# Delta-rule work ahead of the RWKV outputs, and the delta matrix in a weight slab

## What is computed

```python
cols = split_columns(rms_norm_2(x, norm_g[layer]) @ w_in[layer])
y_gdn = gdn_branch(...)     # 6 heads, both directions, chunks: (I + A) U = rhs, then outputs
y_mla = mla_branch(...)     # 6 heads of softmax attention with rotary parts
y_rwkv = rwkv7_branch(...)  # 4 heads, both directions, a linear recurrence
mix = concatenate([y_gdn, y_mla, y_rwkv]) * silu(cols['gate'])
x = x + mix @ w_out[layer]
```

```python
a_mat = beta[..., :, None] * einsum('nhcid,nhcjd->nhcij', k, k) * d_strict
sol = triangular_solve(a_mat, rhs, left_side=True, lower=True, unit_diagonal=True)
p_intra = einsum('nhcid,nhcjd->nhcij', q, k) * d_incl
```

## Time and profile before

| | |
|---|---|
| median of 3 timed runs | 1298.87 us (1296.49 to 1302.06) |
| span of the profiled execution | 1293.0 us; its time with what lies around the span was not recorded |
| TensorE matmul | 1229.4 us busy, 95% |
| VectorE | 755.1 us, 58% |
| ScalarE | 345.7 us, 27% |
| GpSimd | 51.8 us, 4% |
| mean granted TensorE clock | 0.992 of full |

### The profile page before, as it was taken

The page is one execution under the profiler, slowest core; times in us unless marked ns, Lnnn a source line. Parts: engine busy times, 40 slices in busy tenths (PEclk is TensorE's granted clock), DMA queues, the critical chain, the costliest instruction groups (busy, mean ns, idle before and its releaser), DMA issues. The chain is left out here.

```text
span 1293.0 us, 18502 instructions
## 1 busy us (share of the span) xinstructions
PE 1229.4 (95%) x7285; PEld 878.9 (68%) x7285; DVE 755.1 (58%) x1471; ACT 345.7 (27%) x748; POOL 51.8 (4%) x92
## 2 busy tenths in 40 slices
PE   6999899999999999999999999989899999998997
PEld 5877549995447674699844478658566686575683
DVE  3244456775352145676743549884884378858872
ACT  2253312120012144121100222334441231334422
POOL 1100000000000000000000000200300000203000
PEclk9999999999999999999999999999999999999999
DMA  9731105454553431353544433310010632300000
GB/s 296 256 120 66 65 18 207 167 183 146 192 188 126 143 130 66 131 194 136 193 177 151 176 116 130 130 67 2 1 51 1 205 138 81 131 2 1 2 2 33
DMA packets 65853, 149.25 MB, mean 115 GB/s; under 512 B 2097, under 2 KB 8135, under 8 KB 65767
## 3 DMA queue, kind: packets, MB, share of 16 engines
q1 hardware_dynamic: 62432, 141.63, 30.9%
q0 software_dynamic: 1216, 3.52, 1.0%
q10 hardware_dynamic: 2119, 2.91, 0.9%
HBM read 146.95 MB, written 1.07 MB: 114 GB/s over the span
## 5 line engine op out<-in xcount | busy, mean ns | idle before, releaser
L1366 ACT ACTIVATE region<-banks 128x384 f32<-128x384 f32 (+8 forms) x159 | 77.0, 484 | 306.9 <-PE banks L442 105.0
L442 PE MATMUL banks<-hnT,weight_slabs 128*128 128x256 f32 x576 | 126.6, 380 | 3.4 <-DVE hnT L1842 3.4
L442 PEld LDWEIGHTS banks<-hnT,weight_slabs 128*128 128x128 f32 x576 | 108.8, 190 | 20.1 <-DVE hnT L1842 4.1
L494 PE MATMUL banks<-weight_slabs,region 128*128 128x512 f32 x256 | 115.1, 592 | 0.0
L494 PEld LDWEIGHTS banks<-weight_slabs,region 128*128 128x128 f32 x256 | 48.5, 190 | 60.3 <-issue 60.3
L494 PE MATMUL banks<-region 128*128 128x512 f32 x192 | 87.6, 592 | 0.0
L1825 DVE TENSOR_TENSOR region<-weight_slabs 128x1024 f32<-128x1024 f32 x32 | 39.2, 1225 | 80.3 <-PE banks L494 76.4
L1825 DVE TENSOR_TENSOR region<-region 128x256 f32<-128x256 f32 (+23 forms) x160 | 75.8, 474 | 16.9 <-ACT region L1712 11.8
L1983 DVE TENSOR_TENSOR region<-banks,region 128x128 f32<-128x128 f32 x40 | 11.7, 292 | 117.8 <-PE banks L609 91.2
L1825 DVE TENSOR_TENSOR region<-weight_slabs,region 128x1024 f32<-128x1024 f32 x64 | 78.2, 1222 | 1.1
L1322 POOL TENSOR_TENSOR region<-region,consts 128x240 f32<-128x240 f32 (+24 forms) x60 | 34.4, 598 | 955.3 <-DVEq L1834 934.2
(11 more groups left out here) (365 smaller groups left out, 2056.5 us busy)
## 6 DMA issues: line engine op xcount, KB each, us to landing
weight_slabs<-in_mlp_w SPq DMA_DIRECT2D x32, 2048.0 KB, 8.9
weight_slabs<-in_w_in SPq DMA_DIRECT2D x10, 2048.0 KB, 7.7
weight_slabs<-in_od_w_in SPq DMA_DIRECT2D x6, 2048.0 KB, 7.9
weight_slabs<-in_ev_w_in SPq DMA_DIRECT2D x4, 2048.0 KB, 10.9
weight_slabs<-in_w_out SPq DMA_DIRECT2D x4, 2048.0 KB, 8.1
weight_slabs<-in_ev_w_out SPq DMA_DIRECT2D x2, 2048.0 KB, 8.3
weight_slabs<-in_od_w_out SPq DMA_DIRECT2D x2, 2048.0 KB, 7.8
weight_slabs<-in_w_in SPq DMA_DIRECT2D x2, 2016.0 KB, 7.6
```

What stands on the lines that cost most here:

```text
L442: ins = mm(view(ps, b + i * S, (1, S)), view(slabs, o + k * width + c0, (1, P)), view(hnT, k * S, (1, S)), start=k == 0, stop=k == KC - 1)
L494: ins = mm(view(ps, b, (1, 512)), view(R, act + k * st, (1, P)), view(w, wt + k * step_, (1, 512)), start=n == 0 and k == 0, stop=n == 7 a ...
L1366: say(A(dst, view(ps, b, *(dims or ((1, n),)), np_=np_), ACT.Copy, scale=scale), read("scalar", *key))
```

## The change

The change reorders the queues of layers 2 and 3 and moves the delta rule's matrix.

- After `Ur` n = 0 TensorE does `qkss`, `T0`, all four decay groups and `G`. The outputs `Yr` n = 0, `cT` and the right-hand side n = 1 come at ("base", -1) of the delta inversion; `cum`, `Ur` n = 1 and `Yr` n = 1 between its first steps; `uq`, `kv` and `ukv` from step 2 on (`UPS`); the head transposes (`HEADS`) after step 14 and in the first level; all scores in the levels. Most of these now open banks of "five".
- `WARM` loses the points ("base", -1), ("base", 14) and ("X", 2).
- VectorE does `decay_steps(1)` right after the RWKV inversion, into a slab in place of `hn`; `rope` moves from step 2 to step 9, `gate_mul(0, 0)` from 6 to 11, the sums of `Yr` and the decay totals to steps -1, 2, 5 and 6, and `level_matrix(0)` of the delta rule from before the steps to after step 12.
- The delta matrix, the raw intra-chunk matrix and `A` and `X` of the substitution lie in the slot of slab `("out", L, 1)`. SP loads that slab only after three further waits: both intra masks, and the last `Y` bank of the delta inversion.
- ScalarE's queue follows the new order; its square of queries and keys comes ahead of the `RU` copies.

```diff
-        self.M, self.LT, self.ST, self.XT = (GM, GLT, P, XTG) if g else (RM4, RM4 + 4096, 512, XTR)
+        self.LT, self.ST, self.XT = (GLT, P, XTG) if g else (RM4 + 4096, 512, XTR)
         self.QT = self.XT
-        self.A, self.X, self.TMP, self.VT16 = (self.XT + 256 * H + n * 64 * H for n in range(4))
+        self.M, self.A, self.X = (0, 3072, 3456) if g else (RM4, XTR + 256 * H, XTR + 320 * H)
+        self.TMP, self.VT16 = (MIXB + 512, MIXB + 1728) if g else (XTR + 384 * H, XTR + 448 * H)
+        self.ROWS = GP if g else XTR
         self.V64, self.P64, self.Y64 = (GV64, GLT, GLT + 768) if g else (MIXB + 512 * n for n in range(3))
-        self.V16 = GV16 if g else RV16
+        self.V16 = MIXB + 1536 if g else RV16
         self.VTX, self.VX, self.Pk, self.Yk = (GKD, GKD + 384, GC + 1536, GC + 1920) if g else (RKX + 256 * n for n in range(4))
...
+        SC = slot_of[("out", 2, 1)] * SLAB
+        assert slot_of[("out", 3, 1)] * SLAB == SC
+
+        def pair_view(st, off, *dims, **kw):
+
+            return view(slabs, SC + off, *dims, **kw) if st == "g" else view(R, off, *dims, **kw)
+
...
+                if key[0] == "out" and key[1] >= 2 and key[2] == 1:
+
+                    sp.wait_ge(*at("intra_masked", key[1], 0))
+                    sp.wait_ge(*at("intra_backward_masked", key[1], 0))
+                    sp.wait_ge(*at("bank_full", "Y", ("g", key[1]), 2, 1))
...
+                def rwkv_out(n, d):
+                    c, tag = (n, 1 - n)[d], ("r", L, d)
+                    pe.wait_ge(*at("bank_read_by_scalar", "Ur", tag, n))
...
+                rwkv_unit(0)
+                for _ in filler:
+                    pass
+                for _ in first_gate:
+                    pass
+                pe.wait_ge(*at("gdn_squares_ready", L))
+                for i in range(3):
+                    b = open_(("qkss", L, i))
+                    close(mm(view(ps, b, (1, 512)), cc(C_BLK, P), view(R, GP + i * 512, (1, 512)), start=True, stop=True), ("qkss", L, i))
+                rwkv_state()
+                for g in range(4):
+                    decay_group(g)
...
-                SCORES = {("base", 10): 0, ("base", 12): 1, ("Y", 0): 2, ("Z", 0): 3, ("Y", 1): 4, ("Z", 1): 5}
-                PROBS = {("Z", 0): 0, ("Zhalf", 0): 1, ("Y", 1): 2, ("Z", 1): 3, ("VT", 2): 4, ("Z", 2): 5}
+                UPS = {2: 1, 5: 1, 6: 1, 7: 1, 8: 2, 9: 2, 10: 1, 11: 1, 12: 1, 13: 1}
+                HEADS = {("base", 14): 2, ("Y", 0): 2, ("Yhalf", 0): 1, ("Z", 0): 1}
+                SCORES = {("Y", 0): 0, ("Yhalf", 0): 1, ("Z", 0): 2, ("Y", 1): 3, ("Z", 1): 4, ("VT", 2): 5}
+                PROBS = {("Zhalf", 0): 0, ("Y", 1): 1, ("Z", 1): 2, ("Zhalf", 1): 3, ("Z", 2): 4, ("X", 2): 5}
                 VALUES = {("Yhalf", 1): 0, ("Zhalf", 1): 1, ("VT", 2): 2, ("Z", 2): 3}
-                GATES = {("base", 14): 3, ("Yhalf", 0): 2, ("Zhalf", 0): 1, ("Yhalf", 1): 1, ("Zhalf", 1): 1}
-                WARM = (("base", -1), ("base", 14), ("Z", 0), ("Y", 1), ("Z", 1), ("VT", 2), ("Z", 2), ("X", 2))
+                GATES = {("base", 14): 2, ("Yhalf", 0): 2, ("Zhalf", 0): 2, ("Yhalf", 1): 1, ("Zhalf", 1): 1}
+                WARM = (("Z", 0), ("Y", 1), ("Z", 1), ("VT", 2), ("Z", 2))
 
                 def mla_between(what, n):
-                    if what == "base" and n >= 0:
-                        next(up_steps, None)
-                        if n >= 8:
-                            next(heads, None)
+                    if (what, n) == ("base", -1):
+                        for d in range(2):
+                            rwkv_out(0, d)
+                        latents_T()
+                        rwkv_rhs(1)
+                    if (what, n) == ("base", 0):
+                        decay_totals()
+                    if (what, n) == ("base", 1):
+                        rwkv_unit(1)
+                    if what == "base" and n in (3, 4):
+                        rwkv_out(1, n - 3)
+                    if what == "base":
+                        for _ in range(UPS.get(n, 0)):
+                            next(up_steps)
+                    for _ in range(HEADS.get((what, n), 0)):
+                        next(heads)
                     if (what, n) in SCORES:
                         mla_scores(SCORES[what, n])
                     if (what, n) in VALUES:
...
                 invert(("r", L), "r", inverse_between)
+                act.wait_ge(*at("silu_ready", L))
+                say(A(view(R, GP, (1, 1536)), view(R, GC, (1, 1536)), ACT.Square), up("gdn_squares_ready", L))
...
+                rwkv_rhs(1)
+                for d in range(2):
+                    copy_out(view(R, RU + d * 256, (1, 256)), "Ur", ("r", L, d), 1, n=256)
+                act.wait_ge(*at("cum_ready", L))
+                step(A(view(sm, GGA, (12, 2), (1, 12)), view(sm, GCU, (24, 2), (1, 12)), ACT.Exp))
+                say(A(view(sm, GKF, (12, 2), (1, 12)), view(sm, GKF, (12, 2), (1, 12)), ACT.Exp), up("decay_exp_ready", L))
...
-                level_matrix(0)
+                if st == "r":
+                    level_matrix(0)
                 if st == "g":
                     dve.wait_ge(*at("unit_rows_ready", tag[1]))
...
+                    if (st, k) == ("g", 12):
+                        level_matrix(0)
...
+                        go(V.tensor_tensor(view(hn, d * 6 * P, (P, 6), (1, P)) if c == 0 else view(slabs, SC + d * 6 * P, (P, 6), (1, P)), view(cst, C_SI + 2 * (1 - d) * P, (0, 6), (1, P)),
...
                 def gdn_between(what, n):
                     if what == "base":
+                        if n == -1:
+                            for d in range(2):
+                                rwkv_sum(0, d)
                         if n == 2:
+                            decay_totals()
+                        if n in (5, 6):
+                            rwkv_sum(1, n - 5)
+                        if n == 9:
                             rope()
-                        if n == 6:
+                        if n == 11:
                             gate_mul(0, 0)
                     if (what, n) == ("early", 0):
                         mla_max(0)
+                    if (what, n) == ("late", 0):
                         mla_max(1)
-                    if (what, n) == ("late", 0):
+                    if (what, n) == ("Z", 0):
                         mla_max(2)
-                    if (what, n) == ("Z", 0):
-                        mla_max(3)
                         rwkv_variance()
                     if (what, n) == ("early", 1):
+                        mla_max(3)
+                    if (what, n) == ("Z", 1):
                         mla_max(4)
-                    if (what, n) == ("Z", 1):
-                        mla_max(5)
                         intra_mask(1)
                         intra_mask(0)
                     if (what, n) == ("VT", 2):
```

247 lines of the change are left out of this document (110 added, 137 removed).

## The result

| | before | after |
|---|---|---|
| median (lowest to highest), 20 executions each | 1299.11 us (1294.91 to 1303.87) | 1312.09 us (1296.42 to 1342.42) |
| ratio after/before | | 1.0053, 95% interval 1.0032 to 1.0074 |
| span of the profiled execution | 1293.0 us | 1316.2 us (time 1318.01) |
| mean granted TensorE clock in it | 0.992 | 0.969 |

The changed kernel is slower: by 0.53% in the ratio, by 13 us in the medians (the ratio leaves out the executions far above the fastest of their kernel, eight of the changed kernel's twenty, the profiled one among them). Forecast were 1290 us and a range of 1281 to 1299; the measured median lies above the range. Its executions spread over 46 us against 9 us, and the clock spreads with them: 1296.42 us came at a mean granted clock of 0.988, 1308.41 at 0.977, 1342.42 at 0.948. The profiled one lies a little above its median.

A forecast was written before the change was run, and what follows sets the result against it. TensorE, at 95% of the span, bounds the kernel; only its idles, half clock and filler lose time. Stages sum to 91.6 us against 97.9 and 96.6, 11.3 less; minus 2.5 for falls, 9 less: median 1290, range 1281 to 1299.

The forecast's parts named there:

- one fall of the clock more in one or both layers: TensorE's clock in layers 2 and 3: new idles and lost warm-ups bring falls of 1.7 us each, on average 2.5 in all.
- The second rival: Stages 2 and 3: each idle group brings a clock fall, two more a layer, 1.7 us each; 1296 us, no change; chance 0.25.
- lockstep: Delta steps: openings of five shared banks cost TensorE 0.8 us round trips; at 12 a layer 1307 us, slower; chance 0.12.
- Stage 1: From `Ur` 0 to the end of `G`: 14.6 us of work plus 1.3 for a staying clock fall, 15.9 us, now 32.2.
- The first wait: Behind `G`, before `Yr` 0: TensorE idles 1.8 us for the bank VectorE evicts fifth.
- The second wait: Before the head transposes: keys, after `rope` at step 9 and ScalarE's `ukv` evictions, ready at 51.1 us; TensorE idles 3.5.
- Stage 3: From the last of the delta rule's steps to `U`: 40.5 us, with idles of 0.3 at the first `Z` and 1.1 later.
- The total: `Ur` 0 to `U`: 91.6 us a layer against 97.9 and 96.6, 11.3 less together; expected to show as 91 to 94.
- Weights: SP's later load of `out` n = 1: lands in 8.1 us with over 6 us margin, cost 0.
- The picks: GpSimd's 336-column pick took 2262 ns under VectorE's level matrix; changes the sum by nothing while steps follow TensorE.
- The rest around the span: Outside the profiled execution's 1293.0 us span: some 5.9 us up to the timed median of 1298.87, untouched by the change.
- PEclk below 0.95 over the steps: TensorE's clock over the delta steps: below 0.95 in the profile after would show the forecast wrong.

The follow-up runs named there:

- slab-alone kernel: Kernel before plus the slab, its late load and the level matrix after step 12; TensorE's order and warm-ups unchanged: 1294.6 us, ratio 0.9963.
- ninth: Changed kernel with first outputs and second right-hand side back in front of `G`, `cT` and the four query products ahead of the steps: 1343.3 us.
- twelfth: Changed kernel with `cT` ahead of first outputs, four query products between these and the second right-hand side, two lost warm-up points back: 1345.7 us.
- sixteenth: Kernel before with the slab; first outputs, second right-hand side, decay totals, second `Ur` and second outputs behind `G` after the query products, later key/value products: 1305.4 us.

## Why the prediction was wrong

**The step that failed** is the term of the sum "one fall of the clock more in one or both layers ... 1.7 each, on average 2.5 in all". In the profiled execution, falls in the two layers took 57.9 us against 10.2, a loss of (57.9 - 10.2)/2 = 23.9 us. At the median clocks of all executions, 0.988 and 0.975, the same reckoning gives (0.025 x 1312) - (0.012 x 1299) = 17 us, against the 2.5 put in. I had sized a fall by the earlier trace rows, one of 3.4 us as a stage mean of 0.95 implied, and gave each new one that price. The runs show that long falls begin at waits and that their length is another matter: 10 us in layer 2 and 38 in layer 3 behind the same 2.11 us, with the same products. The second rival, "the clock eats it", had the mechanism and the sign of the loss, but used the same price of 1.7 us, and so ended at 1296. No case reached the side where the result lies by this road; slower had 0.12, for a lockstep that did not come (in layer 2 TensorE waits 0.40, 0.35, 0.25 and 0.54 us between the last `Yr` and step 14, and no more).

**Stage 1** was walked at 14.6 us plus 1.3 for a fall. `G` ended after 14.2 us in both layers of the profiled execution; the fall of the earlier trace rows was absent from both, so "the fall stays" was wrong here, to the good.

**The first wait**, 1.8 us at the bank evicted fifth, was right: 2.11 us. The eviction starts 1.23 us behind the start of `G` and takes 4.32, as in the earlier trace rows; `G` was 2.86 us of work where the sum had 3.0.

**The second wait**, keys at 51.1 us: the first head starts at 930.64 - 874.41 = 56.2 in layer 2, less 5.1 lost to its fall of 10.2 us, 51.1. The row of L446 at 1215.27 shows the same wait in layer 3, ended by ScalarE's `ukv` copies, as said. It idles 0.25, 0.54 and 1.35 us, 2.1 where 3.5 was walked, and 0.75 for VectorE's rows; the unforeseen wait of 1.50 us for the totals' bank lies before it. That the sum met 51.1 to a tenth is in part luck.

**Stage 3**, 40.5 us: 972.76 - 930.64 = 42.1 in layer 2. Of the 1.6 us more, 1.1 is the wait at the first `Z`: 1.44 us for ScalarE (L437 in the waits), not 0.3.

**The total** in layer 2 at equal clock is 98.35 - 5.1 = 93.2 against the walk's 91.6, inside the "91 to 94" of the last part; in layer 3 the same reckoning gives 114.76 - 23.9 = 90.9, so it is good to some 2 us. It also shows a smaller miss: at equal clock the two layers took (96.6 - 1.7) + (97.9 - 3.4) = 189.4 us before and 184.1 after, 5.3 less, where the walk without its falls had 2 x 90.3 = 180.6, 8.8 less. Without any new fall the kernel would have come out, by estimate, at 1299 - 5.3 = 1294, the upper end of the forecast's own 1285 to 1294. Of the marks in the prediction's last part, the one for being wrong came true: PEclk below 0.95 over the steps, 0.87 and 0.63.

**Weights** cost nothing, as predicted. The late load landed in 8.4 us (8.1 in the earlier trace rows) and no product waited for it; the group that first reads that slab follows its predecessor without a gap:

```profile
weight_slabs<-in_w_out SPq DMA_DIRECT2D x4, 2048.0 KB, 8.4
```
```profile
1276.35 3.65 PE L1238 MATMUL banks<-weight_slabs,hnT 128*128 128x512 f32 x8
```

**The picks.** With the level matrix gone from under it, the 336-column pick takes 748 ns, not the 2262 of the earlier trace rows:

```profile
L1351 POOL TENSOR_TENSOR region<-weight_slabs,consts 128x336 f32<-128x336 f32 x2 | 1.5, 748 | 0.0
```

The Trainium skill (SBUF — State Buffer, SBUF: two separate sides) has a two-input VectorE instruction and a reading GpSimd one exclude each other, and this agrees. The prediction gave that no weight in the sum, and for the changed kernel rightly; in the slab-alone kernel the 2.0 us of waits for picks did go.

**The rest around the span** was put at 5.9 us. The changed kernel's twenty executions and those of the kernel before have 1.7 to 1.9 us around it; the other 4.1 were the clock of the profiled execution, 0.992, against 0.988 in the median one. The medians already told that this kernel's time varies with its clock.

**What stays open.** The runs do not show what ends a fall, nor why the same wait ahead of the same products opens one in one layer and none in the other. It ended in 288-column products in the changed kernel (1201.7) and did not in the ninth and twelfth. Nor is it settled why three warm-up points, apart from the one ahead of `U`, matter on the slab-alone kernel and were of no use on the changed one, or how the late keys and the late emptying of the totals' bank share their 7 us. A mended order was not tried: the sixteenth's head, the totals emptied after step 1, late keys and eight warm-up points together.

## What to carry to other kernels

Before moving narrow products together, ask what keeps TensorE's clock: here the same instructions took 38.6 or 50.5 us. Price a possible fall by the length of the stretch that follows the wait, not by the last fall that was seen. A wait of 1.3 to 2.1 us ahead of the steps could cost nothing or a fall of 51 us, so put work that need not wait there, as the sixteenth kernel does behind `G` (1305.4 us), and take more than one execution before believing a trace; and test the parts of a change by themselves, since here one of them, the slab with the level matrix moved, paid (1294.6 us) inside a change that lost.
